# One more quarter of the convolution's output product in the fifth attention step

## What is computed

```python
q, k, v, glu, g_att, g_conv = jnp.split(z, splits, axis=-1)
o = _diff_attention(q, k, v, lam, cid)          # 8 heads, two softmaxes each
y_att = (_rms(o, subln_w[l]) * (1.0 - lambda_init)).reshape(b, lp, ATT_V)
u = glu[..., :CONV_CH] * jax.nn.sigmoid(glu[..., CONV_CH:])
u = _causal_dwconv(u, conv_dw_w[l], conv_dw_b[l])
u = jax.nn.silu(_layernorm(u, conv_ln_w[l], conv_ln_b[l]))
y_conv = u @ w_conv_out[l]
m = jax.nn.sigmoid(g_att) * y_att + jax.nn.sigmoid(g_conv) * y_conv
h = h + m @ w_out[l]
```

## Time and profile before

| | us |
|---|---|
| median of 3 executions | 1832.05 |
| lowest, highest | 1831.72, 1833.18 |
| the profiled execution | 1831.8 |
| its span in the trace | 1830.0 |
| TensorE busy in the span | 1803.4 (99%) |
| VectorE busy | 1347.5 (74%) |
| ScalarE busy | 921.1 (50%) |
| the attention's 32 steps | about 358 to 477 in the span |

### The profile page before, as it was taken

One profiled execution on the slowest core, in us unless ns is written; L12 is line 12 of the kernel. 1 busy time (PEld: TensorE's weight loads), 2 busy tenths in 40 slices (PEclk: granted clock), 3 DMA queues, 4 the chain that ended last, 5 costly groups with the idle time before them and its releaser, 6 DMA issues.

```text
span 1830.0 us, 32898 instructions
## 1 busy us (share of the span) xinstructions
PE 1803.4 (99%) x13738; PEld 1720.8 (94%) x13738; DVE 1347.5 (74%) x2384; ACT 921.1 (50%) x1788; POOL 128.6 (7%) x110
## 2 busy tenths in 40 slices
PE   8999999999999999999999999999999999999998
PEld 7999999978899998999899999999899999999987
DVE  5888897678757773566688787978458888787844
ACT  6223333578735432343456666666337566666632
POOL 0000000000000000000011121211000111121000
PEclk9999999999999999999999999999999999999999
DMA  5322222201122223222357777775322677777431
GB/s 178 100 81 92 93 93 70 93 24 39 56 98 93 87 77 114 93 84 74 98 122 152 168 154 155 159 153 128 120 93 78 127 156 154 153 153 154 114 126 69
DMA packets 229474, 202.46 MB, mean 111 GB/s; under 512 B 5846, under 2 KB 225807, under 8 KB 229326
## 3 DMA queue, kind: packets, MB, share of 16 engines
q1 hardware_dynamic: 177566, 174.67, 30.9%
q0 software_dynamic: 51744, 25.70, 11.4%
q10 hardware_dynamic: 16, 0.00, 0.0%
HBM read 198.25 MB, written 2.10 MB: 109 GB/s over the span
## 4 chain that ended last, share of the span: by engine, by line
PE 89%; DVE 5%; ACT 4%; issue 1%; DMA 0%; DVEq 0%; SPq 0%; ACTq 0%
PE ps L195 62%; PE ps L199 25%; PE ps L204 2%; DVE wlo L210 1%; ACT p L207 1%; DVE ast L1062 1%; ACT whi L207 0%; DVE sw L210 0%; DMA xt<-in_x_dram 0%; ACT nhi L207 0%; DVE kr L210 0%; DVE qr L210 0%; DVE na L210 0%; DVE tf L218 0%; ACT ones_d L207 0%
## 5 line engine op out<-in xcount | busy, mean ns | idle before, releaser
L210 DVE TENSOR_TENSOR wlo<-raw,whi 128x1024 fp32r<-128x1024 f32 (+1 forms) x357 | 424.2, 1191 | 257.9 <-ACT whi L207 256.3
L207 ACT ACTIVATE whi<-raw 128x1024 fp32r<-128x1024 f32 (+1 forms) x357 | 367.0, 1030 | 264.1 <-PE ps L195 219.4
L195 PE MATMUL ps<-nhi,whi 128*128 128x256 f32 (+3 forms) x1840 | 406.5, 289 | 4.4 <-DVE nlo L210 2.1
L195 PE MATMUL ps<-nhi,wlo 128*128 128x256 f32 (+3 forms) x1840 | 402.7, 287 | 0.0
L195 PE MATMUL ps<-nlo,whi 128*128 128x256 f32 (+3 forms) x1712 | 365.6, 286 | 0.0
L195 PEld LDWEIGHTS ps<-nhi,whi 128*128 128x128 f32 x1840 | 296.8, 189 | 8.6 <-DVE nlo L210 2.3
L195 PEld LDWEIGHTS ps<-nhi,wlo 128*128 128x128 f32 x1840 | 296.0, 190 | 2.1
L195 PEld LDWEIGHTS ps<-nlo,whi 128*128 128x128 f32 x1712 | 271.6, 189 | 1.9
L199 PE MATMUL ps<-thi,whi 128*128 128x256 f32 x784 | 224.6, 286 | 0.4 <-ACT pa L207 0.2
L199 PE MATMUL ps<-thi,wlo 128*128 128x256 f32 x784 | 221.6, 283 | 0.0
L199 PE MATMUL ps<-tlo,whi 128*128 128x256 f32 x784 | 221.5, 282 | 0.0
(11 more groups left out here) (323 smaller groups left out, 3172.2 us busy)
## 6 DMA issues: line engine op xcount, KB each, us to landing
raw<-in_w_in_dram SPq DMA_DIRECT2D x90, 1024.0 KB, 5.8
raw<-in_w_up_dram SPq DMA_DIRECT2D x22, 1024.0 KB, 5.0
raw<-in_w_out_dram SPq DMA_DIRECT2D x20, 1024.0 KB, 5.0
s1t<-in_w_in_dram SPq DMA_DIRECT2D x49, 256.0 KB, 3.0
s1t<-in_w_in_dram POOLq DMA_DIRECT2D x49, 256.0 KB, 7.2
raw<-in_w_in_dram POOLq DMA_DIRECT2D x49, 256.0 KB, 4.7
raw<-in_w_down_dram SPq DMA_DIRECT2D x8, 768.0 KB, 4.3
raw<-in_w_down_dram SPq DMA_DIRECT2D x8, 640.0 KB, 4.0
```

The costliest lines, as they stand in the source:

```text
L195: return pe.put(after, lambda e: e.matmul(o, w, m, start=start, stop=stop_), mark)
L207: return ac.put(after, lambda e: e.activation(o, i, func, **kw))
L210: return dv.put(after, lambda e: e.tensor_tensor(o, a, b, op))
```

## The change

EARLY gets a fifth entry, 1. Step 4 takes a quarter where QUARTERS[0] gave it none. All later steps take as many as before, but each quarter of the list is taken one place earlier: quarter 3 of a tile in r = 1, quarter 0 of the next in r = 2, quarters 1 and 2 in r = 3. The list is empty after step 29; step 30 takes none, and spare_bank has its third bank from step 30 on instead of 31.

```diff
@@ -1032,7 +1032,7 @@
 
             ORDER = (1, 2, 0, 3)
             QUARTERS = (0, 1, 1, 2)
-            EARLY = (0, 0, 1, 1)
+            EARLY = (0, 0, 1, 1, 1)
 
             def head(i):
                 t = ORDER[i % 4]
```

## The result

The changed kernel takes 1836.72 us (median of 10 executions, 1836.02 to 1837.29) against 1832.2 us for the kernel before (10 executions): a ratio of 1.0025 with a 95% interval of 1.0017 to 1.0033, slower by 4.5 us. The forecast was 1836.5. Its profiled span is 1834.4 us against 1830.0.

A forecast was written before the change was run, and what follows sets the result against it. TensorE, 99% busy, was taken to bind narrowly over the VectorE and ScalarE chain; 1.38 + 3.75 - 0.99 + 0.33 = +4.47 us gave 1836.5 us, range 1833.9 to 1838.9.

The forecast's parts named there:

- step 4's quarter, less what it fills: Steps 4 and 5 on TensorE: the added quarter costs 1.61 us, 0.23 of waiting vanishes, the 0.83 wait stays: +1.38.
- handover of step 7: Bank 7 between quarters 1 and 2: TensorE waits for VectorE's multiply, 0.75 us each, five on its path, +3.75.
- four periods from step 11 to 27: Attention heads on TensorE: four handovers of 0.75 us add 3.00, less 0.99 of absorbed waits.
- last head: Before step 31's scores: ScalarE's exponentials come 0.33 us later through step 27's handover, +0.33; bounds -0.45 and +0.75.
- What the delay absorbs: Steps 11 to 27: with TensorE 0.75 us late, its waits for ScalarE before r = 3 scores go, -0.99.
- The missing quarter: Step 30, left without a quarter: gives nothing back, because step 31's scores wait about 1.35 us for ScalarE's exponentials.
- hidden: Rival, r = 3 pairs: handover costs nothing, exponentials come sooner, quarter comes back: -1.22 us, 1830.8; chance 0.07.
- lengthened by a late VectorE: Rival, r = 3 pairs: maximum and "ga" delay VectorE's multiply, 1.1 us per handover: +6.22, 1838.3; chance 0.11.
- The quarter is returned: Rival, step 31: scores not held by ScalarE, TensorE regains 1.61 us, pays the sixth handover: +3.28, 1835.3; chance 0.16.

## Why the prediction was right

The sum was 4.47 us and 4.52 was measured (4.48 in the traces), but that is closer than the terms were, two of which were off by about 0.2 in opposite directions:

| term | forecast | in the trace |
|---|---|---|
| step 4's quarter, less what it fills | 1.38 | 1.18 |
| handover of step 7 | 0.75 | 0.75 |
| four periods from step 11 to 27 | 3.00 - 0.99 = 2.01 | 2.05 |
| last head | 0.33 | 0.50 |

- *Step 4's quarter.* The mechanism held: scores to transposes fell from 1.11 to 0.88, and the wait of 0.83 moved along unchanged. The quarter was mis-sized. I took 1.61, from its start to the next scores, but this includes the passage to the scores, which was there already after the values. Scores of step 4 to scores of step 5 grew from 1.87 to 3.30: 1.43.
- *The handover* is as built: 0.32 + 0.48 - 0.13 + 0.10 = 0.77 from the rows above. The profile shows each as a wait of 0.52, not 0.65: the last matmul is still in flight for 0.28 of the 0.80. The experiments show it as the cause: without the multiply it is gone, with work between it is covered, and without the pairs the loss shrinks to 0.9.
- *What the delay absorbs.* The waits of 0.2 vanished as forecast, but the reason given, that TensorE comes 0.75 later, was not the one that counts, so this size was right in part by luck. They vanish too where TensorE isn't made late: without the multiply (14.46) and with the multiply behind the next combine and maximum (14.45 to 14.49). What held the chain was VectorE's stand before the multiply, which the prediction named only for its rival and for a bound. In the changed kernel nothing stands ahead of step 28's combine any more: its reciprocal starts 5.36 after step 27's scores (468.68 after 463.32), against 6.21 before (465.61 after 459.40). That ScalarE's exponential of r = 3 was behind the waits, which I took up for the experiments, was wrong.
- *The missing quarter.* It gave nothing back, as forecast. TensorE waited 0.85 before step 31's scores where 1.35 was forecast, and 0.21 before step 30's values (the forecast had "may wait 0.3"): together 1.06. The sizes as measured give 0.16 + 1.43 for the quarter - 0.82 for step 27's handover (step 27's scores to step 28's are 6.58, 463.32 to 469.90, against 5.76, 459.40 to 465.16) + 0.50 = 1.27. The 0.2 that is left is, by an estimate, how idle time is counted: a wait shows only from the end of the matmul in flight, 0.16 after the next could have started (0.28 less 0.12), and here there are two.
- *The last head* was 0.17 longer than forecast. Most of that is there by step 29: VectorE's reciprocal was forecast 0.33 later and came 0.43 later, 10.45 into the head (473.77) against 10.02 before (469.42), behind ScalarE's exponentials of step 28. ScalarE's exponential of step 30 then starts 0.47 later, 14.26 into the head (477.58) against 13.79 before (473.19). In the changed kernel VectorE has the multiply "m" at 475.85 as well as "mlo" at 476.19 ahead of that block's maximum, where it had "mlo" alone, but between the exponentials of steps 29 and 30 only 0.04 are added (475.97 to 477.58, against 471.62 to 473.19).
- *The rivals.* The handover was neither hidden nor lengthened by a late VectorE. In step 7 the maximum ended at 391.55, just as the multiply's turn came (391.53), and added nothing. "The quarter is returned" (1835.3) fell to the wait of 0.85.

## What to carry to other kernels

When a list of pieces is shifted by one, look for pieces that now meet. Here two accumulations into the same PSUM bank, one right behind the other, cost TensorE the whole turn through the evacuating engine, about 0.75 us, and 1 us of other matmuls between them covered it from step 11 on. An engine that has an instruction waiting for the end of another's long piece holds back all that is queued behind it: moving that one multiply behind the next maximum took 0.25 to 0.3 us from each period of the kernel before. And where two chains are nearly tied, as here within 0.25 us, a quarter taken from one of them at the end returned nothing.

## What the runs showed of the hardware

In 4 of the 12 profiled executions TensorE's granted clock fell to its lower level for about 3.4 us, beginning between 374.5 and 375.5 us: each time within the last five matmuls of step 3's quarter, and on through step 4's own work. No other stretch of the attention had it. Three windows around it in the kernel without the multiply, then the middle one in the changed kernel, which did not have it:

```profile
374.00:375.50 1.50, 1.50 (x13) 1.49 (x13) 0.84 (x3) 1.50 (x4) 0.00 (x0) 1.00 0.00 0
375.50:378.90 3.40, 3.40 (x17) 2.51 (x16) 2.01 (x5) 0.44 (x3) 0.00 (x0) 0.51 0.00 0
378.90:380.50 1.60, 1.60 (x14) 1.47 (x13) 0.41 (x1) 1.29 (x6) 0.00 (x0) 0.98 0.00 0
```

```profile
376.00:379.40 3.40, 3.40 (x28) 2.81 (x26) 3.07 (x8) 1.72 (x8) 0.00 (x0) 1.00 0.00 0
```

The mean of 0.51 in the second window is the lower level, 1.2 GHz of 2.4. Ahead of it lie steps 1 to 3, where TensorE waits several times (0.8 us for "ones_d", 0.6 for "m") and works in small pieces. From the first matmul of step 3's quarter to step 5's scores the four have 6.45 to 6.49 us, the changed kernel 4.94 (374.46 to 379.40): 1.5 us for one such piece, a third of what this change cost. All four executions were of kernels with a quarter in step 4, out of nine profiled with one and three without; the fall begins before that quarter is issued, so these runs don't show that the two are connected. Executions of one kernel spread by 1.2 to 2.5 us in these measurements. The mean granted clock over the whole span is on record for most of them: of the kernel before's 83 beside the experiments, the 7 at 0.998 average 1833.1 us and the 76 at 0.999 average 1832.1. So a lower clock somewhere goes with 1 us more, in the kernel without a quarter in step 4 too. Where in the span it lay, only the profiled executions show, so whether this piece is the reason for the spread stays open.
